# Last up projection of a two-block transformer kernel: one product of 512 columns for both parts of the tokens, a PSUM bank per tile half

## What is computed

```python
def conv_ffn(h, w_up, conv_w, conv_b, w_down):
    S = h.shape[1]
    u, g = jnp.split(h @ w_up, 2, axis=-1)
    u_pad = jnp.pad(u, ((0, 0), (CONV_WIDTH - 1, 0), (0, 0)))
    u = sum(conv_w[tap] * u_pad[:, tap:tap + S] for tap in range(CONV_WIDTH)) + conv_b
    return (jax.nn.gelu(u) * g) @ w_down
```

## Time and profile before

| what | value |
|---|---|
| median of the runs | 820.37 us |
| profiled execution | 821.45 us |
| its span, first to last instruction | 819.6 us |
| granted clock of TensorE, mean | 1.000 |
| PE busy | 804.7 us, 98% |
| DVE busy | 609.3 us, 74% |
| ACT busy | 453.5 us, 55% |
| POOL busy | 96.5 us, 12% |

### The profile page before, as it was taken

How to read it: one execution, slowest core, us unless ns; L and a number is a source line. 1 busy time by engine, 2 the same in 40 slices (tenths; PEclk the granted TensorE clock), 3 DMA queues, 4 the chain that set the end, 5 groups by cost and what they waited for, 6 DMA issues and landing times.

```text
span 819.6 us, 12095 instructions
## 1 busy us (share of the span) xinstructions
PE 804.7 (98%) x4841; PEld 697.8 (85%) x4841; DVE 609.3 (74%) x967; ACT 453.5 (55%) x804; POOL 96.5 (12%) x106
## 2 busy tenths in 40 slices
PE   7999999999999999999999999999999999999997
PEld 6878888888888888889998778788888999999886
DVE  6878776978777855567669777958577799998734
ACT  6656556645545634445475656664387655554533
POOL 4100000000000000000400000000000555654100
PEclk9999999999999999999999999999999999999999
DMA  9854644556665555554966343365633555555551
GB/s 326 239 162 152 197 150 154 162 173 192 224 201 180 182 203 183 177 205 114 258 203 206 104 129 130 103 154 180 203 106 115 194 170 190 185 176 196 180 189 51
DMA packets 81640, 143.40 MB, mean 175 GB/s; under 512 B 5123, under 2 KB 35873, under 8 KB 81585
## 3 DMA queue, kind: packets, MB, share of 16 engines
q1 hardware_dynamic: 79264, 137.11, 51.5%
q0 software_dynamic: 2160, 5.46, 2.3%
q10 hardware_dynamic: 160, 0.07, 0.0%
HBM read 141.05 MB, written 1.05 MB: 173 GB/s over the span
## 4 chain that ended last, share of the span: by engine, by line
PE 92%; DVE 4%; ACT 3%; issue 0%; DMA 0%; ACTq 0%; DVEq 0%
PE PS L1318 89%; PE PS L1332 3%; ACT WK_f L1941 1%; DVE low_r L2451 1%; ACT high L1944 1%; DMA VR<-in_norm_attn_g_dram 0%; ACT WK_f L1944 0%; DVE WK_f L2455 0%; DVE WK_f L2459 0%; DVE XN L2451 0%; DVE XN L2459 0%; DVE HT_r L2451 0%; DVE AR_f L2459 0%; ACT L1938 0%; DVE X L2451 0%
## 5 line engine op out<-in xcount | busy, mean ns | idle before, releaser
L2451 DVE TENSOR_TENSOR low_r<-low_f,high 128x1024 fp32r<-128x1024 f32 (+1 forms) x256 | 325.8, 1315 | 75.8 <-ACT high L1944 75.4
L1944 ACT ACTIVATE high<-low_f 128x1024 fp32r<-128x1024 f32 (+1 forms) x264 | 257.3, 1024 | 78.6 <-DMA low_f<-in_w_down_dram 34.8
L1318 PE MATMUL PS<-HT_r,high 128*128 128x256 f32 (+2 forms) x1232 | 267.5, 308 | 0.0
L1318 PE MATMUL PS<-high,AR_r 128*128 128x512 f32 (+2 forms) x724 | 214.7, 377 | 0.0
L1318 PEld LDWEIGHTS PS<-HT_r,high 128*128 128x128 f32 (+1 forms) x1232 | 199.6, 190 | 12.3
L1318 PE MATMUL PS<-HT_r,low_r 128*128 128x256 f32 (+1 forms) x712 | 200.9, 282 | 0.0
L1318 PE MATMUL PS<-high,HT_r 128*128 128x512 f32 (+1 forms) x576 | 189.6, 397 | 1.0 <-DVE HT_r L2451 0.7
L1318 PEld LDWEIGHTS PS<-high,AR_r 128*128 128x128 f32 (+1 forms) x724 | 129.1, 181 | 26.3 <-issue 0.5
L1318 PEld LDWEIGHTS PS<-HT_r,low_r 128*128 128x128 f32 (+1 forms) x712 | 135.2, 190 | 0.0
L1318 PE MATMUL PS<-low_r,AR_r 128*128 128x512 f32 (+2 forms) x362 | 133.9, 374 | 0.0
L1318 PEld LDWEIGHTS PS<-high,HT_r 128*128 128x128 f32 x576 | 108.2, 190 | 25.4 <-issue 2.7
(11 more groups left out here) (174 smaller groups left out, 675.8 us busy)
## 6 DMA issues: line engine op xcount, KB each, us to landing
low_f<-in_w_in_dram SPq DMA_DIRECT2D x39, 1024.0 KB, 5.2
low_f<-in_w_up_dram SPq DMA_DIRECT2D x38, 1024.0 KB, 5.2
low_f<-in_w_down_dram SPq DMA_DIRECT2D x27, 1024.0 KB, 4.9
low_f<-in_w_out_dram SPq DMA_DIRECT2D x8, 1024.0 KB, 5.0
low_f<-in_w_xkv_dram SPq DMA_DIRECT2D x4, 1024.0 KB, 5.6
low_f<-in_w_branch_gla_dram SPq DMA_DIRECT2D x2, 1024.0 KB, 5.0
low_f<-in_w_branch_nsa_dram SPq DMA_DIRECT2D x4, 512.0 KB, 6.0
low_f<-in_w_xq_dram SPq DMA_DIRECT2D x2, 1024.0 KB, 5.2
```

The source lines that it names most:

```text
L1318: return nc.tensor.matmul(o, l, r, start=start, stop=stop, skip_group_check=True)
L1944: return nc.scalar.activation(o, i, ACT.Copy, bias=0.0, scale=1.0)
L2451: return nc.vector.tensor_tensor(o, a, b, op)
```

## The change

Each half h of a tile gets a bank of its own, and a tile a pair of banks, from a ring of four pairs (`upair`). The high part of the weights meets high and low tokens in one product of 512 columns; eight of these are followed by eight of 256 columns (low part of the weights, high tokens) into the first half of the bank. So the sum of a tile lies in two halves of the bank: ScalarE copies the second (`cross_u`, `cross_g`) to SBUF (in XN), VectorE adds the first (`sum_u`, `sum_g`). The middle tap, the taps and the product with the gate now read SBUF. GpSimd's five instructions for the gelu stay and are two steps. The list for a period is written out by hand (`UP2`, `UP2_END`), a digit being how many periods behind j a step is, and the splits of units are in it too, two units ahead of their use. For j = 0 the turn of tile (0,0) stands ahead of tile (0,1).

```diff
+UP2 = ("high0 low0 low0 tile00 cross_g1 gelu_poly1 sum_g1 tile01 high0 gelu_tanh1 gelu_out1 low0 cross_u0 "
+       "sum_u0 conv_mid0 gated1 ffn_hi1 conv_taps0 low0 ffn_rest1 tile10 tile11 ")
+UP2_END = ("cross_g1 sum_g1 gelu_poly1 high low low gelu_tanh1 gelu_out1 high gated1 ffn_hi1 ffn_rest1 low low "
+           "low low low ")
...
+    def gated_tiles(self, order, j):
+        for word in order.split():
+            name, n = word.rstrip("0123456789"), word[len(word.rstrip("0123456789")):]
+            if name == "high":
+                if self.n_split < min(len(self.plan), self.n_done + NSLOT):
+                    self.step("split_hi", u=self.n_split, parts=(0, 1))
+                    self.n_split += 1
+            elif name == "low":
+                self.half_low()
+            elif name == "tile":
+                p, h = int(n[0]), int(n[1])
+                if j == p == 0:
+                    if h == 1:
+                        self.step("upt_turn")
+                    continue
+                if h == 0:
+                    self.upair(("up2", j, p))
+                u = self.n_done
+                assert self.plan[u][0] == "up2" and self.n_low > u
+                self.step("up2_m", j=j, p=p, u=u, h=h)
+                if h == 1:
+                    self.done(self.U["up2", j, p].full)
+            elif 0 <= j - int(n) < 11:
+                self.step(name, j=j - int(n))
...
+    def upair(self, key):
+        n = self.rings.get("upair", 0)
+        self.rings["upair"] = n + 1
+        return self.use(key, ((6, 7), (0, 1), (2, 3), (4, 5))[n % 4])
...
+        self.fbank(("up2", 0, 0))
         for j in range(11):
...
+            self.gated_tiles(UP2, j)
+        self.gated_tiles(UP2_END, 11)
         self.lows()
...
# TensorE, up2_m
-                m = turned(bank(use)[:, 256 * h:256 * h + 256], s["u"], 128 * h, 8, "up2")
+                o, w = PS[:, use.banks[h], :], weights(s["u"])[:, :, 128 * h:128 * h + 128]
+                for k in range(8):
+                    pe.wait_ge(s_hi, 2 * s["u"] + k // 4 + 1)
+                    if k % 4 == 0:
+                        columns_ready("up2", k)
+                    mm(o, w[:, k, :].hi, HTP[:, k, :, :].rearrange("p a n -> p (a n)"), k == 0, False)
+                for k in range(8):
+                    unit_ready(s["u"], k)
+                    m = mm(o[:, 0:256], w[:, k, :].lo, HT.hi[:, k, :], False, k == 7)
...
# ScalarE
+            def cross_u(s):
+                j = s["j"]
+                use = U["up2", j, 0]
+                act.wait_ge(*use.full)
+                if j > 2:
+                    act.wait_ge(s_um, j - 1)
+                if j == 0:
+                    cp(ublock(0), halves(bank(use))).then_inc(use.read[0], 1)
+                else:
+                    cp(ublock(j), PS[:, use.banks[0]:use.banks[0] + 2, 256:512]).then_inc(s_ub, 1)
...
+            def cross_g(s):
+                j = s["j"]
+                use = U["up2", j, 1]
+                act.wait_ge(*use.full)
+                if j > 1:
+                    act.wait_ge(*U["up2", j - 2, 1].read)
+                    act.wait_ge(s_ff, j - 1)
+                cp(gblock(j), PS[:, use.banks[0]:use.banks[0] + 2, 256:512]).then_inc(s_gb, 1)
...
# VectorE
+            def sum_u(s):
+                j = s["j"]
+                use = U["up2", j, 0]
+                if j == 0:
+                    return
+                dve.wait_ge(s_ub, j)
+                tt(ublock(j), PS[:, use.banks[0]:use.banks[0] + 2, 0:256], ublock(j), ALU.add).then_inc(use.read[0], 1)
...
                 for h in range(2):
                     ch = 2 * j + h
-                    u = bank(use)[:, 256 * h:256 * h + 256]
-                    stt(Um[:, h, 1:256], u[:, 0:255], CW[:, 1, ch:ch + 1], Um[:, h, 1:256], ALU.mult,
-                        ALU.add).then_inc(*own.up())
-                    dve.wait_ge(*own.now())
-                    m = stt(Um[:, h, 2:256], u[:, 0:254], CW[:, 0, ch:ch + 1], Um[:, h, 2:256], ALU.mult, ALU.add)
-                m.then_inc(use.read[0], 1)
+                    m = stt(Um[:, h, 1:256], u[:, h, 0:255], CW[:, 1, ch:ch + 1], Um[:, h, 1:256], ALU.mult, ALU.add)
+                m.then_inc(*own.up())
+                dve.wait_ge(*own.now())
+                for h in range(2):
+                    ch = 2 * j + h
+                    m = stt(Um[:, h, 2:256], u[:, h, 0:254], CW[:, 0, ch:ch + 1], Um[:, h, 2:256], ALU.mult, ALU.add)
+                m.then_inc(s_um, 1)
...
+            def sum_g(s):
+                j = s["j"]
+                use = U["up2", j, 1]
+                Um = wk(1024 * (j % 3), 2, 256)
+                dve.wait_ge(s_gb, j + 1)
+                tt(gblock(j), PS[:, use.banks[0]:use.banks[0] + 2, 0:256], gblock(j), ALU.add).then_inc(use.read[0], 1)
+
+            def gated(s):
+                j = s["j"]
+                dve.wait_ge(*U["up2", j, 1].read)
+                dve.wait_ge(s_yg, j + 1)
+                tt(FT[:, 2 * j:2 * j + 2, :].f, wk(1024 * (j % 3) + 512, 2, 256), gblock(j), ALU.mult).then_inc(s_ff, 1)
...
```

More of the change, by code:

```diff
@@ L278, in pairs_of_banks, with half_low @@
         return self.use(key, ((4, 5), (0, 1), (2, 3))[n % 3])
+    def gated_tiles(self, order, j):
[22 more added lines that the diff above has]
+                self.step(name, j=j - int(n))
+    def half_low(self):
+        if self.n_low < self.n_split:
+            part = 1 if self.low_begun else 0
+            self.step("split_lo", u=self.n_low, parts=(part,))
+            self.n_low += part
+            self.low_begun = not part
+    def upair(self, key):
+        n = self.rings.get("upair", 0)
+        self.rings["upair"] = n + 1
+        return self.use(key, ((6, 7), (0, 1), (2, 3), (4, 5))[n % 4])
     def fbank(self, key):
@@ L992, in run @@
         self.cross(queries)
+        self.fbank(("up2", 0, 0))
         for j in range(11):
[L994 to L1010, removed]
+            self.gated_tiles(UP2, j)
+        self.gated_tiles(UP2_END, 11)
         self.lows()
-        self.step("up2_t", j=10)
         main = self.given("down2", self.rows("down2", 22))
@@ L1101, in halves, with ublock, gblock @@
             return ap.rearrange("p (a n) -> p a n", a=2)
+        def ublock(j):
+            return halves(XN[:, j % 2, 0:512])
+        def gblock(j):
+            return halves(XN[:, j % 2, 512:1024])
         G = [VC[:, 0, 8 * j:8 * j + 8] for j in range(6)]
@@ L1233, in two_blocks @@
         s_zcross = sem("z_cross")
-        s_uc, s_yt, s_yh, s_yg, s_fh, s_f, s_fin = (
-            sem(n) for n in ("conv_mid", "gelu_poly", "gelu_tanh", "gelu", "ffn_hi", "ffn_lo", "final"))
+        s_ub, s_gb, s_uc, s_um, s_yt, s_yh, s_yg, s_ff, s_fh, s_f, s_fin = (
+            sem(n) for n in ("up2_cross", "gate2_cross", "conv_mid", "conv", "gelu_poly", "gelu_tanh", "gelu", "ffn",
+                             "ffn_hi", "ffn_lo", "final"))
         S = Schedule(A, full, read, s_unit)
@@ L2409, in up2_c @@
                 Um = wk(1024 * (j % 3), 2, 256)
-                act.wait_ge(*use.full)
+                act.wait_ge(*use.read)
+                u = ublock(j)
                 if j >= 3:
-                    act.wait_ge(*U["up2", j - 3, 1].read)
+                    act.wait_ge(s_ff, j - 2)
                 act.wait_ge(*U["xv", 3].read)
@@ L2416, in up2_c, with gelu_tanh @@
                     ch = 2 * j + h
-                    m = fn(Um[:, h, :], bank(use)[:, 256 * h:256 * h + 256], ACT.Identity, scale=CW[:, 2, ch:ch + 1],
-                           bias=CB[:, ch:ch + 1])
+                    m = fn(Um[:, h, :], u[:, h, :], ACT.Identity, scale=CW[:, 2, ch:ch + 1], bias=CB[:, ch:ch + 1])
                 m.then_inc(s_uc, 1)
[L2421 to L2427, removed]
+            def gelu_tanh(s):
                 j = s["j"]
@@ L2431, in up2_g, with ffn_hi @@
                 fn(Y, Y, ACT.Tanh, scale=GELU_C).then_inc(s_yh, 1)
+            def cross_g(s):
[6 more added lines that the diff above has]
+                cp(gblock(j), PS[:, use.banks[0]:use.banks[0] + 2, 256:512]).then_inc(s_gb, 1)
+            def ffn_hi(s):
+                j = s["j"]
+                o = FT[:, 2 * j:2 * j + 2, :]
+                act.wait_ge(s_ff, j + 1)
+                cp(o.hi, o.f).then_inc(s_fh, 1)
             nc.scalar.dma_start(cst[:, 0:NFIRST], A["shape_constants"][:, 0:NFIRST]).then_inc(s_id, 16)
@@ L3197, in up2_c, with ffn_rest @@
                     ch = 2 * j + h
-                    u = bank(use)[:, 256 * h:256 * h + 256]
-                    stt(Um[:, h, 1:256], u[:, 0:255], CW[:, 1, ch:ch + 1], Um[:, h, 1:256], ALU.mult,
-                        ALU.add).then_inc(*own.up())
-                    dve.wait_ge(*own.now())
-                    m = stt(Um[:, h, 2:256], u[:, 0:254], CW[:, 0, ch:ch + 1], Um[:, h, 2:256], ALU.mult, ALU.add)
-                m.then_inc(use.read[0], 1)
-            def up2_t(s):
```

(12 more changed lines are left out.)

15 lines of the change are left out of this document (9 added, 6 removed).

## The result

The changed kernel takes **821.95 us** (median of 13 runs, 820.94 to 823.18) against 820.36 (13 runs, 820.03 to 821.24) for the kernel before in the same comparison: ratio 1.0021, 95% interval 1.0012 to 1.0029. It is slower by 1.6 us, 0.2%, where I had forecast 818.0 and 2.4 us faster. The profiled execution took 823.17 us around a span of 821.3; that is 1.2 above its median, as the profiled one of before is 1.1 above its own, and the two spans are 1.7 us apart. All of that arises from tile (0,1) on: TensorE is free for it at 632.81 before and at 632.66 after.

A forecast was written before the change was run, and what follows sets the result against it. TensorE was taken to bound the kernel, with VectorE only just keeping up; -4.4 saved, +0.6 at the turn and +1.4 of waiting gave -2.4 us, hence 818.0 us against 820.4, range 816.3 to 826.3.

The forecast's parts named there:

- 4.4 - 0.6 = 3.8: TensorE in the last up projection: 4.4 us saved by 512-column products over 42 halves, less 0.6 lost at the turn.
- the turn: At j = 0, TensorE idles before tile (0,1) for ScalarE's copy, earlier hidden by the first half: 0.6 us lost.
- Where TensorE waits: Before the down projection, TensorE arrives at 750.5, waits for j = 9's sum of g until 751.9: 1.4 us.
- The layout's start (640.4): VectorE's first fourth low part in the last up projection cannot start before about 640.4 us.
- nine periods of 11.6: VectorE's period, laid out by turns with GpSimd, is 11.6 us against TensorE's 11.10; nine lead to j = 9.
- at nothing: ScalarE gains two copies a period, 0.59 us each, reaching some 65% busy; this was taken to cost no time.
- A: Rival: GpSimd's last product goes before the queued low part, period 12.6, TensorE waits 9.4 us: 826.0 us; 22%.
- B: Rival: VectorE's period is 11.44 or less, so TensorE's whole 3.8 us gain shows: 816.6 us; 20%.
- C: Rival: TensorE keeps the alternating pace of the first up projection, 1.6 us saved and hardly a wait: 818.8; 10%.
- D: Rival: GpSimd's first product ends 1.16 us after the low part, period 11.98, waits 4.9 us: 821.5; 18%.
- The threshold: TensorE starts to wait ahead of the down projection at a VectorE period of 11.44; each further 0.1 us costs 0.9.
- Taps from SBUF: VectorE's taps and product with the gate last as long from SBUF; the skill's figures implied some 0.3 us a period less.

The follow-up runs named there:

- run 2: Changed kernel with GpSimd's five instructions of a period cut to 16 of 512 columns, order of work kept: 817.82 us, against 820.43 for the kernel before.
- Run 5: Changed kernel with a small tanh on ScalarE behind the first middle taps, so tanh's table loads early: 820.16 us, ratio 1.0000 to the kernel before.
- run 1: Changed kernel with bank pairs in another order, so the down projection first opens banks that held tile (9,0), not (9,1): 821.38 us.
- Run 7: Changed kernel with early tanh table, other bank order, turn back between tile (0,1)'s halves, and the polynomial's square on ScalarE right behind the taps: 816.62 us.
- run 8: Changed kernel with GpSimd's instructions cut to 16 of 512 columns and products of 512 and 256 columns alternating instead of eight and eight: 818.97 us.
- run 3: Kernel before the change with GpSimd's five instructions cut to 16 of 512 columns: 820.32 us, ratio 0.9998 to the uncut kernel before.
- run 4: Changed kernel with the polynomial's square moved from GpSimd to ScalarE, queued behind tile (j, 0): 818.88 us, runs in two groups.
- run 6: Changed kernel with early tanh table load, other bank order, and the turn of tile (0,0) back between the halves of tile (0,1): 820.45 us.

## Why the prediction was wrong

**TensorE's saving held, less one term.** I had 4.4 - 0.6 = 3.8 without waits. From TensorE being free for tile (0,1) to the first product of the down projection it is 754.19 - 632.81 = 121.38 us before and 750.52 - 632.27 = 118.25 in run 2: 3.1 saved. The term that was too good is the step of the 512s: taken at 0.227 us from the earlier trace rows, measured 0.230 (eight from 692.24 to 694.08 take 1.84; the mean over run 2's stage is the same). 336 products by 0.003 are 1.0 us; the 256s, at 0.119 on average, give 0.3 back. The grouped pace and the turn (0.6, measured 0.5: 633.49 - 632.66, less the 0.36 that the turn itself takes, 635.69 to 636.05 before) were right.

**The step that failed is "Where TensorE waits": the sum of g of j = 9 done at 751.9.** It ends at 753.49 + 0.68 = 754.17:

```profile
753.49 0.68 DVE L2515 TENSOR_TENSOR XN<-PS,XN 128x512 f32<-128x512 f32 x1
```

The layout's start (640.4) and the stretch from a fourth low part to that sum (7.07, measured 7.04) held. Between them stood nine periods of 11.6; there were one of 12.7 and eight of 11.76. The 1.1 of the first is ScalarE's table load, which I cost "at nothing" together with ScalarE's copies, by its busy share. The load is part of the 63.5 us of the earlier trace rows and stood in the trace of before at 640.12, but a share says nothing about an order. The 8 x 0.16 are GpSimd's last product: I let it end 0.90 us behind the low part, as one first product had done, and it ends 1.16 behind it; the product with the gate then waits for it and the taps with that. Run 5 confirms the first (1.3 us earlier), run 2 that all of it hangs on GpSimd's work beside VectorE's.

**Only one wait was counted.** VectorE, 2.3 us later, leaves its low parts late as well, one inside the stage (748.40) and those of the down projection. I stopped at bank 2; run 1, where the bank is no longer in the way, shows 1.00 and 0.77 us of waits for low parts in its place. And in about half of the executions, to judge by their mean clock, slow products follow the long wait, which I had not thought of. Sum by the traces: 3.1 saved; from 632.66 to 754.27 it is 121.61 us, so the waits up to the down projection cost 121.61 - 118.25 = 3.4 where I had 1.4; slow products 1.6. That is +1.9, with +1.8 between the two traces (183.11 - 181.30) and +1.6 between the medians.

**The rivals.** A (order lost, 826.0) falls: the low part at 707.06 goes first and lasts 1.21. B (whole gain) falls in the change. Run 7 has B's number, 816.6, but by another sum: it removes a GpSimd product and also has the turn's 0.5 us back. C (alternating pace) falls; run 8 is what it would look like. D (821.5) has nearly the time that came out, but only half by its mechanism: GpSimd's first product lasts 1.96 at 700.24 and ends 0.90 behind the low part, as laid out. D's 1.16 is there, but at the last product, where it lengthens the period by 0.16, not 0.38; the rest of the time has other sources (the table load, the slow products, TensorE's smaller gain). A right number is no proof of a rival. The threshold was right: at 0.9 us for each 0.1 of period, 0.16 and a long first period were enough to undo the gain.

**Taps from SBUF.** Taps and product with the gate read SBUF now, and last as before: four taps to the next instruction 1.70 us (700.08 - 698.38), a tap of 254 columns 480 ns on average where the earlier trace rows had 482 from PSUM, and the product with the gate 0.69 us where it was 0.68. By the Trainium skill, "VectorE: DVE Perf Modes", section on the TRN2 errata, they should have been shorter; no row shows it, and the measurement decides.

## What to carry to other kernels

Where one engine has half a per cent to spare, lay out its queue over the first and the last period too, not only a middle one: a table load or a late weight there delays every period behind it, and it comes due wherever the buffers end, more than once. A stage that another engine bounds hides contention for free (run 3). Make that engine faster, and the first thing to remove is the contention (here one GpSimd product moved to ScalarE, at the moment when ScalarE is free), not the place where the wait shows. In this kernel products of equal shape are best put behind one another (run 8).

## What was unexpected of the hardware

- A GpSimd instruction can lose its turn to VectorE: the same scalar step took 0.75 us or 3.02 us behind the same VectorE instructions with the same offset (run 4). What decides it stays open.
- TensorE's clock fell in some executions behind a long wait. In the changed kernel, after 2.36 us: granted clock 0.55, six steps of 512 columns at 0.425 us (754.84 to 757.39), the lower of its levels, 1.2 GHz. In run 5 it fell in the profiled execution from 754.5 on, 1.5 us behind the end of a wait of 1.82. It did not in the profiled ones of runs 1 and 6, where waits were 1.0 us or less, nor in that of run 4 behind 1.26 us. By the Trainium skill, "TensorE: Matmul & The Clock Gate", Part 1, 512 columns take 426.7 ns at the lower level, and the trace agrees; its 215.7 ns at full clock is below the 230 shown here.
- The table load is 1.28 us and tanh starts 0.02 behind it (646.65 + 1.28 = 647.93, then 647.95). The Trainium skill, "ScalarE: Activation LUTs", What ACT_TABLE_LOAD costs, adds about 1.38 us of drain to it; no row here shows that.
- One and the same kernel differs by about 1 us from run to run before this stage is even reached: tile (0,1) starts at 633.49 in the trace of the changed kernel and at 632.45 in that of run 1, whose steps up to there are the same but for the banks. So small effects were read inside the stage.
